# Modulation products on the unsplit fp32 slab, in four column quarters

## The reference, cut to what matters

```python
for l in range(DEPTH):
    mod_p = _adaln(cond_ctx, w_mod[l], b_mod[l])   # silu(c_ctx) @ w_mod[l] + b_mod[l], cut in six
    mod_s = _adaln(c, w_mod[l], b_mod[l])          # the same for the latent stream
    hp = _modulate(xp, norm1_g[l], mod_p[0], mod_p[1])
    ...
    xp = xp + mod_p[2] * out_p
```

## Time and profile before

| | |
|---|---|
| median of three runs (lowest, highest) | 3123.11 us (3122.1, 3124.43) |
| span of the profiled execution | 3109.4 us |
| what lies between span and median | 13.7 us |
| TensorE matmuls busy | 2846.1 us (92%), 15164 records |
| TensorE weight loads busy | 2255.3 us (73%) |
| VectorE busy | 2058.5 us (66%) |
| ScalarE busy | 1622.1 us (52%) |
| DMA, mean over the span | 196 GB/s |

### The profile page before, as it was taken

The page is one execution under the profiler, slowest core; times in us unless marked ns, Lnnn a source line. Parts: engine busy times, 40 slices in busy tenths (PEclk is TensorE's granted clock), DMA queues, the critical chain, the costliest instruction groups (busy, mean ns, idle before and its releaser), DMA issues. The chain is left out here.

```text
span 3109.4 us, 43571 instructions
## 1 busy us (share of the span) xinstructions
PE 2846.1 (92%) x15164; PEld 2255.3 (73%) x15164; DVE 2058.5 (66%) x2347; ACT 1622.1 (52%) x1916; POOL 1.8 (0%) x9
## 2 busy tenths in 40 slices
PE   6699976888999999999997999857888999999998
PEld 2377755666777777778885778546677888888887
DVE  6866646577777777777667774243467666667674
ACT  5555522455666666666554664212244555555554
POOL 0000000000000000000000000000000000000000
PEclk9899987998999999999998999667799999999998
DMA  9788810675888888886554885102254666665562
GB/s 327 266 274 270 271 61 17 201 251 187 266 274 266 274 266 272 266 273 204 191 164 164 264 277 166 34 16 83 75 169 143 189 189 188 187 187 189 165 213 82
DMA packets 325512, 607.93 MB, mean 196 GB/s; under 512 B 23458, under 2 KB 38268, under 8 KB 325116
## 3 DMA queue, kind: packets, MB, share of 16 engines
q1 hardware_dynamic: 324876, 603.86, 60.5%
q10 hardware_dynamic: 432, 2.23, 0.2%
q0 software_dynamic: 64, 0.00, 0.0%
HBM read 601.38 MB, written 4.63 MB: 195 GB/s over the span
## 5 line engine op out<-in xcount | busy, mean ns | idle before, releaser
L390 DVE TENSOR_TENSOR w_lo<-raw,w_hi 128x1024 fp32r<-128x1024 f32 x1140 | 1370.3, 1222 | 737.5 <-ACT w_hi L383 732.2
L383 ACT ACTIVATE w_hi<-raw 128x1024 fp32r<-128x1024 f32 x1140 | 1170.2, 1054 | 928.1 <-PE banks L511 856.2
L510 PE MATMUL banks<-xs_ffn,w_hi 128*128 128x512 f32 x4224 | 1493.7, 396 | 15.0 <-DVE xs_ffn L689 14.1
L511 PE MATMUL banks<-xs_ffn,w_lo 128*128 128x256 f32 x4224 | 1187.8, 281 | 0.0
L510 PEld LDWEIGHTS banks<-xs_ffn,w_hi 128*128 128x128 f32 x4224 | 797.9, 189 | 216.2 <-issue 16.0
L511 PEld LDWEIGHTS banks<-xs_ffn,w_lo 128*128 128x128 f32 x4224 | 794.6, 188 | 5.5
L470 PE MATMUL banks<-w_hi,cond_split 128*4 128x512 f32 x768 | 305.6, 398 | 25.1 <-DVE w_lo L390 17.7
L470 PE MATMUL banks<-w_lo,cond_split 128*4 128x512 f32 x768 | 305.3, 398 | 0.0
L510 PE MATMUL banks<-xs_even,w_hi 128*128 128x512 f32 x576 | 209.0, 401 | 7.4 <-DVE xs_even L689 7.3
L510 PE MATMUL banks<-xs_out,w_hi 128*128 128x512 f32 x512 | 186.3, 403 | 8.2 <-DVE xs_out L719 8.2
L510 PE MATMUL banks<-xs_odd,w_hi 128*128 128x512 f32 x512 | 185.8, 401 | 7.4 <-DVE xs_odd L689 7.1
(11 more groups left out here) (309 smaller groups left out, 2028.0 us busy)
## 6 DMA issues: line engine op xcount, KB each, us to landing
raw<-in_w_mod SPq DMA_DIRECT2D x384, 512.0 KB, 4.8
raw<-in_ffn_w_up SPq DMA_DIRECT2D x352, 512.0 KB, 4.1
raw<-in_ffn_w_down SPq DMA_DIRECT2D x176, 512.0 KB, 4.3
raw<-in_even_w_in SPq DMA_DIRECT2D x72, 512.0 KB, 4.6
raw<-in_odd_w_in SPq DMA_DIRECT2D x64, 512.0 KB, 4.6
raw<-in_even_w_out SPq DMA_DIRECT2D x32, 512.0 KB, 5.1
raw<-in_odd_w_out SPq DMA_DIRECT2D x32, 512.0 KB, 4.0
raw<-in_odd_w_in SPq DMA_DIRECT2D x8, 448.0 KB, 3.3
```

The costliest lines, as they stand in the source:

```text
L383: act.activation(w_hi[:, s % SPLIT], raw[:, s % RAW], ACT.Copy).then_inc(hi_done.sem, 1)
L390: dve.tensor_tensor(w_lo[:, s % SPLIT], raw[:, s % RAW], w_hi[:, s % SPLIT].bitcast(F32), ALU.subtract).then_inc(lo_done.sem, 1)
L510: pe.matmul(bank, w_hi[:, slot, c, cols], moving[:, c, :], start=start and c == 0, stop=False)
L511: mm = pe.matmul(bank[:, 0:NT], w_lo[:, slot, c, cols], moving[:, c, 0:NT], start=False, stop=stop and c == CHUNKS - 1)
```

## The change

The mod slabs are no longer split. `mod_products` multiplies the loaded slab `raw` itself in plain fp32: one matmul for each chunk instead of two, with the conditioning padded by zeros to 32 columns (`cond`). The chunks of a group, numbered 0 to 15, are dealt to four quarters of TensorE's columns: chunk n writes rows 32 (n mod 4) and on of the bank. The copy takes all 128 rows, and the turning matmuls sum over 128 rows by a constant with ones at rows 0, 32, 64, 96 (and 1, 33, 65, 97). TensorE waits for the landing of a mod slab; its slot is free for the next load when TensorE has multiplied it (`mod_used`). The rings `w_hi` and `w_lo` now hold own slabs alone, so the split runs four *own* slabs ahead.

```diff
+QUAD = 32
+QUADS = P // QUAD
...
-        c[stream, C_SUM + stream] = 1.0
-        c[2 + stream, C_SUM + stream] = 1.0
+        c[stream::QUAD, C_SUM + stream] = 1.0
...
-        cond_split = sb("cond_split", [P, KD, 4], F32R)
-        mod_rows = sb("mod_rows", [4, 2, SLABW])
+        cond = sb("cond", [P, KD, QUAD])
+        mod_rows = sb("mod_rows", [P, 2, SLABW])
...
         def load_slab(sp, f, i, s, in_slot_before):
             slot = s % RAW
-            wait(sp, hi_done.sem, in_slot_before)
-            wait(sp, lo_done.sem, in_slot_before)
+            what, count = in_slot_before
+            if what == "own":
+                wait(sp, hi_done.sem, count)
+                wait(sp, lo_done.sem, count)
+            else:
+                wait(sp, mod_used.sem, count)
...
         def split_stream(eng, f, split, places, also=None, left=()):
...
-                for s in range(f.slabs):
+                for s, (kind, g, k) in enumerate(f.seq):
                     run_pieces(f, places, i, s, first, left)
-                    ahead = s + SPLIT
+                    if kind == "mod":
+                        continue
+                    ahead = f.own_at.index(s) + SPLIT
...
+            if not owns:
+                for o in range(SPLIT):
+                    split(eng, f.next, 0, o)
...
                 for s, (kind, g, k) in enumerate(f.seq):
-                    pe.wait_ge(lo_done.sem, f.slab(i, s) + 1)
                     if kind == "mod":
-                        products = mod_products(pe, f, i, s, g, k)
+                        pe.wait_ge(*slab_landed(f, i, s))
+                        mod_products(pe, f, i, s, g, k).then_inc(mod_used.sem, 1)
                     else:
+                        o = f.own_at.index(s)
+                        pe.wait_ge(lo_done.sem, f.own(i, o) + 1)
...
             for c in range(CHUNKS):
-                for n, half in enumerate((w_hi, w_lo)):
-                    mm = pe.matmul(banks[0:4, MOD_ROWS + j % 2, :], cond_split[:, CHUNKS * k + c, :],
-                                   half[:, s % SPLIT, c, :], start=(k == 0 and c == 0 and n == 0),
-                                   stop=(k == MOD_SLABS - 1 and c == CHUNKS - 1 and n == 1))
+                n = CHUNKS * k + c
+                quad = QUAD * (n % QUADS)
+                mm = pe.matmul(banks[quad:quad + QUAD, MOD_ROWS + j % 2, :], cond[:, n, :], raw[:, s % RAW, c, :],
+                               start=n < QUADS, stop=n >= KD - QUADS)
...
-            act.activation(mod_rows[:, j % 2, :], banks[0:4, MOD_ROWS + j % 2, :], ACT.Copy).then_inc(rows_out.sem, 1)
+            act.activation(mod_rows[:, j % 2, :], banks[:, MOD_ROWS + j % 2, :], ACT.Copy).then_inc(rows_out.sem, 1)
...
-                    for s in range(SPLIT):
-                        split_hi(act, first, 0, s)
...
+                    dve.memset(cond[:], 0.0).then_inc(dve_step.sem, 1)
...
-                    for s in range(SPLIT):
-                        split_lo(dve, first, 0, s)
```

More of the change, by code:

```diff
@@ L155, in __init__ @@
         self.slabs = len(self.seq)
+        self.own_at = [s for s, slab in enumerate(self.seq) if slab[0] == "own"]
+        self.mod_at = [s for s, slab in enumerate(self.seq) if slab[0] == "mod"]
         self.ends = [self.seq.index(("own", g, per_group - 1)) for g in range(groups)]
@@ L158, in __init__, with own, mod_slab, used @@
         self.by_halves = by_halves
-        self.slab0 = self.group0 = self.mod0 = self.half0 = 0
+        self.own0 = self.group0 = self.mod0 = self.half0 = 0
         self.slot0 = [0] * RAW
-        self.before = [0] * RAW
+        self.before = [("own", 0)] * RAW
         self.next = None
         self.continues = False
-    def slab(self, i, s):
-        return self.slab0 + i * self.slabs + s
+    def own(self, i, o):
+        return self.own0 + i * len(self.own_at) + o
+    def mod_slab(self, i, m):
+        return (self.mod0 + i * self.mods) * MOD_SLABS + m
+    def used(self, i, s):
+        if self.seq[s][0] == "own":
+            return "own", self.own(i, self.own_at.index(s)) + 1
+        return "mod", self.mod_slab(i, self.mod_at.index(s)) + 1
     def group(self, i, g):
@@ L185, in plan @@
 def plan(phases):
-    slab = group = mod = half = 0
-    held, last = [0] * RAW, [0] * RAW
+    own = group = mod = half = 0
+    held, last = [0] * RAW, [("own", 0)] * RAW
     for n, ph in enumerate(phases):
-        ph.slab0, ph.group0, ph.mod0, ph.half0 = slab, group, mod, half
+        ph.own0, ph.group0, ph.mod0, ph.half0 = own, group, mod, half
         ph.slot0, ph.before = list(held), list(last)
@@ L195, in plan @@
             if k:
-                last[slot] = slab + (ph.iters - 1) * ph.slabs + slot + RAW * (k - 1) + 1
-        slab += ph.iters * ph.slabs
+                last[slot] = ph.used(ph.iters - 1, slot + RAW * (k - 1))
+        own += ph.iters * len(ph.own_at)
         group += ph.iters * ph.groups
@@ L364, in body @@
                 for s in range(RAW, f.slabs):
-                    load_slab(sp, f, i, s, f.slab(i, s - RAW) + 1)
+                    load_slab(sp, f, i, s, f.used(i, s - RAW))
                 if last:
@@ L370, in body @@
                         newest = s + RAW * (f.loads_of(s) - 1)
-                        load_slab(sp, f, i + 1, s, f.slab(i, newest) + 1)
+                        load_slab(sp, f, i + 1, s, f.used(i, newest))
             rolled(sp, f.iters, body)
@@ L453, in body @@
                         if f.by_halves:
-                            products = slab_products(i, s, g, k, out if k == 0 else 0)
+                            products = slab_products(i, o, g, k, out if k == 0 else 0)
                         else:
-                            products = slab_products(i, s, g, k)
-                    products.then_inc(slab_used.sem, 1)
+                            products = slab_products(i, o, g, k)
+                        products.then_inc(slab_used.sem, 1)
                     run_pieces(f, places, i, s, first, left)
@@ L486, in turn_mod @@
                 mm = pe.matmul(banks[:, MOD_COLS + j % 2, 2 * t:2 * t + 2], mod_rows[:, j % 2, P * t:P * t + P],
-                               const[0:4, C_SUM:C_SUM + 2], start=True, stop=True)
+                               const[:, C_SUM:C_SUM + 2], start=True, stop=True)
             mm.then_inc(rows_turned.sem, 1)
@@ L517, in split_products, with one @@
         def split_products(pe, f, operand, ready, left):
-            def one(i, s, g, k, out):
-                ready(i, s)
-                return tile_products(pe, s % SPLIT, f.first_bank(g), operand(s, k), k == 0, k == f.per_group - 1, out)
+            def one(i, o, g, k, out):
+                ready(i, o)
+                return tile_products(pe, o % SPLIT, f.first_bank(g), operand(o, k), k == 0, k == f.per_group - 1, out)
             return product_stream(pe, f, one, left)
@@ L735, in ahead, with ready @@
                     before[name](eng)
-            def ready(pe, f, i, s):
-                kind, g, k = f.seq[s]
+            def ready(pe, f, i, o):
+                kind, g, k = f.seq[f.own_at[o]]
                 if "ready" in before and f is phases[0] and isinstance(i, int) and i == 0 and g == 0:
@@ L792, in _ @@
                         else:
-                            left = split_products(pe, f, operands[n], lambda i, s, f=f: ready(pe, f, i, s), left)
+                            left = split_products(pe, f, operands[n], lambda i, o, f=f: ready(pe, f, i, o), left)
                     for _, call in left:
@@ L799, in group_used @@
         def group_used(f, i, g):
-            return f.slab(i, f.ends[g]) + 1
+            return f.own(i, f.per_group * (g + 1) - 1) + 1
         def half_banks(f, g, n):
```

38 lines of the change are left out of this document (17 added, 21 removed).

## The result

The changed kernel takes 3148.19 us (median of four runs, 3141.70 to 3150.74), the kernel before beside it 3122.61 (3114.30 to 3124.43). The ratio is 1.0088, with a 95% interval of 1.0070 to 1.0107: slower, as forecast, by under 1% but clear of the noise. The difference is 25.6 us, where the prediction's sum had 16. The profiled span is 3148.8 us.

A forecast was written before the change was run, and what follows sets the result against it. TensorE, busy 923.93 of 924 us in the long stretch, was taken as the bound. Products +41, turning -11 and phase starts -14 gave +16 us: span 3109.4 to 3125, plus 13.7 to the median, 3139 us; range 3040 to 3230.

The forecast's parts named there:

- The signs: Expected in the changed profile: two records per chunk, overlapping chunk starts, 1.2 us per single or double slab, three waits gone, 756 splits.
- single slabs: Mod slabs alone between own slabs on TensorE: 0.86 us plus 0.35 for shape and lag, each losing 0.28 us.
- double slabs: Two mod slabs at a group's end: four chunks in four quarters take as long as two, each gaining 0.65 us.
- turning: Turning matmuls lose their own two shape changes, the mod slab's way out falls on them: 40 x 0.28 = -11 us.
- phase starts: TensorE's three long waits for a split go, plus some clock loss regained: -14 us, bounds -5 and -17.
- program start: TensorE starts some 4.9 us earlier, but the first phase's end needs two more landings: zero, plus or minus 3 us.
- rival 2: The quarters do not overlap: a single slab 2.00 us, a double 3.72, some 3450 us in all; chance 0.23.
- Rival 1: The array's change of shape is free: a group's mod products take 6.02 to 6.79 us, say 3056 in all; chance 0.20.
- a lag: Delay between overlapping chunks in different quarters: 0.07 us added to the 0.28 for shape, giving 0.35 us a visit.
- upper bound, 0.59: Highest price for going out of the array's shape and back, from half-clock changes between 128 and 64 rows: 0.59 us.
- Loads: SyncE's loads run at most eight slabs ahead, 15 us; landing takes 4.8 and the split 2.3, so it costs nothing.

The follow-up runs named there:

- e1: The kernel before, run once more unchanged: 3123.71 us.
- e8: The changed kernel with both chunks of a mod slab, and all four of a double one, in one quarter of the columns: 3436.05 us.
- e9: The changed kernel with a 128-column stationary operand, still plain fp32, so mod products keep the array's full shape and every chunk fills the whole bank: 3375.54 us.
- e10: The kernel before with slabs dealt by twos (own, own, mod, mod) and the turning behind the next group's first mod pair: 3125.11 us.
- e7: The changed kernel in its own order, with the split running three own slabs ahead instead of four: 3137.03 us.
- e4: The changed kernel with slabs dealt by twos, so four visits of four chunks in a group instead of seven: 3176.82 us, 1.019 of the kernel before.
- e2: The kernel before with an unused tile of 1792 bytes, putting operands at the changed kernel's addresses: 3114.14 us.
- e3: The changed kernel with an unused tile of 256 bytes, giving operands the kernel before's offset within 2 KB: 3150.21 us.

## Why the prediction was right, and where its sum was off

The signs came as listed but for one, the double slab's cost: two records a chunk, 7 ns between chunks, 1.18 us for the single slab (1.21 predicted), no waits at 146, 722 and 1684, 756 splits. The terms, by the starts of all records of a kind (against e1, which has the same cost per slab as the kernel before):

| term | predicted, us | measured, us |
|---|---|---|
| 240 single slabs | 240 x 0.28 = +67 | 240 x (1.185 - 0.931) = +61 |
| 40 double slabs | 40 x -0.65 = -26 | 40 x (1.676 - 1.863) = -7 |
| turning | -11 | 40 x (0.89 - 1.175) = -11 |
| phase starts | -14 | -18 |
| program start | 0 | -2 |
| sum | +16 | +23 |
| between the two profiled spans of like pace | | +27 |

**The quarters and the shape's price.** Right: rival 2 would have been e8, and 3436 us is what the prediction gave it (3450). Rival 1 falls with the 0.31 us between e8 and e9; the earlier trace rows gave 0.28. The 0.07 us that the prediction added for a lag is not there (7 ns): the price is a little higher than it was taken and the lag is nothing, so that 1.21 is near 1.18 partly by luck. Its upper bound, 0.59 from the earlier trace rows, was misread: by the starts of the single records, the two of one shape stand 0.59 us apart there and those across a change of rows 0.56, so that row shows no price at the change. That the earlier trace rows shows none says nothing of the quarters: a visit in fp32r with four columns is free (e10), one in plain fp32 with 32 is not. The Trainium skill, "PSUM — Partial Sum Buffer", The four PSUM rules, notes that float32r matmuls force the mask of all column groups; e10, without a price for leaving the array's shape, and e8, with one, agree with it.

**The double slab: the term that was mis-sized.** The prediction gave it 1.21 us and a gain of 26 us; it has 1.68 and 7. The shorter visit no longer covers the copy and the sum of the own banks, which 1.86 us covered before. The step behind it is "Loads": "landing takes 4.8 us and the split 2.3, so nothing". The distance of eight slabs that it counted on is the ring's, but the split, now four own slabs ahead, asks for its slab eight slabs ahead too, so nothing of it is left. SyncE issues that load behind the load of a mod slab, which waits until TensorE has used the mod slab just ahead of the present own one; landing takes 3.9 us, the own slab 2.8, and the split stands 1.4 to 1.6 us. No product needs that split soon, so the prediction's "only if landings took over 12 us" holds for the products; but the copy is queued behind it. e7 shows it, since there the wait goes with the order and the products unchanged; e4 shows it grown.

**Phase starts.** From a phase's first own matmul to the first of its ninth own slab were 37.5, 38.2 and 37.1 us in the three phases with a wait, and are 32.9, 32.6 and 33.6 with dearer slabs: 13.8 us less, and with the 1.3 us by which a group's mod slabs are dearer (6 x 0.25 less 0.19), three times, 18. That is a little over the upper bound of 17, and the clock's part is in it (the earlier trace rows and its answer above).

**Program start and turning.** The first own product comes at 133.2 us for 134.9; the turning, alone, fell by 0.285 us, as said.

**What is left.** 27.0 less 23 is 4 us, and three differences that no term had make it up (3.0 + 2.7 - 1.2). 3.0 us are the slower own pace in the down projection of layer 0's feed-forward part (679 pairs), where e1 has the fast one. 2.7 lie in the five long stretches behind the first own product in which no own pair runs, 534.9 us in all for 532.2 in e1; they took 532.8 in e2 (the kernel before) and 533.2 in e3 (the changed one), so most of this may be a difference between executions. And the phase at 562 us, which had no wait, took 32.6 us in e1 and 32.7 in the changed kernel up to its ninth own slab, though its mod slabs are dearer by 1.3, so that some 1.2 are gained there: from 565 to 570 us the clock was 0.71 in e1 and 1.00 in the changed kernel. What sets these three is open.

**How much was luck.** The sum's 16 and the measured 23 are near each other because misses of both signs meet: the double slab is 19 us dearer than the prediction had it, the single slabs 6 cheaper, the phase starts 4 and the program's start 2. Without the wait that "Loads" put at nothing the terms would come to some +4 and the spans to some +8, at the edge of the 6 us that the prediction takes for no change. e7 agrees: its span is 13.4 us above e1's, and 10.9 of them are the waits that came back at phase starts. So the mechanism, overlapping quarters and a price of the shape by visit, was right by its reasons; that the kernel came out clearly slower it owes to a wait that the prediction had ruled out.

## What to carry to other kernels

Here a small matmul that leaves the array's shape pays for the visit (0.31 us), not for the slab: put as many chunks as there are quarters side by side, and count visits. When work is taken from an in-order engine, ask what the remaining work now asks for earlier: a split that runs as far ahead as the ring is deep stands in front of everything queued behind it, urgent copies above all. And a slow stretch is also a cover; what a shorter one uncovers belongs in the sum.

## What the hardware showed that was not expected

- Own pairs, in stretches with nothing but own slabs, run at one of two paces, 348.9 or 353.3 ns, at a granted clock of 1.00, whatever the kernel; in the three longest such stretches the pace holds throughout, but for their first products, and can differ from one to the next in one execution (353.3 and then 348.9 in e4 and e10). Between mod slabs the mean is 350.5 to 352.7 in every kernel. What sets it is open. Between the profiled executions of before and e1 it makes 9.2 us; that it makes the spread of the other runs of the kernel before (3109.5 to 3125.3) is likely and not shown.
- Four plain fp32 chunks of 512 columns in four quarters cost 1.20 us in and out, and 3.75 in one quarter (e8): nearly all of the fourfold. The Trainium skill, "TensorE: Matmul & The Clock Gate", Part 3, has 2.38x for three column tiles. No run here has three; for four, less the 0.31 us for the shape, the rows give 3.44 to 0.89 us, 3.9x.
- The time of a run is 1.8 to 1.95 us above its span in these runs; the 13.7 us between the span and the median of the kernel before were a difference between executions.
